# The Mamba branch's convolution projection: twelve column slabs regrouped into three groups of four slabs of two k tiles

## The chip, the cores and the metric

The kernel runs on one core of a Trainium2 chip. The metric is the device time of one execution in microseconds (us). A profiled execution has its own time; the profile's span is the stretch from its first to its last instruction.

## The reference

Four layers act on a sequence of 512 positions by 1024 features in fp32: two of a three-branch block (gated spatial mixing, Mamba2, differential attention, then a feed-forward network) and two of a second block. Only the first block's layers ("first layer" and "second layer" below) hold the code that is changed. What matters of them:

```python
h = rmsnorm(x, attn_norm_g[layer])
proj = h @ w_in[layer]                      # 1024 -> 8208 columns
gm_u, gm_v, ssm_z, ssm_xbc, ssm_dt, da_q, da_k, da_v, gates = split_cols(proj, IN_SIZES)
...
xbc = jax.nn.silu(causal_dwconv(xbc, conv_w, conv_b))    # 1536 columns, 4 taps along the sequence
dt = jax.nn.softplus(dt_raw.astype(jnp.float32) + dt_bias.astype(jnp.float32))
y = ssd_scan(xs..., dt, a_log, bm..., cm..., d_skip)
return rmsnorm(y * jax.nn.silu(z), norm_g)
```

## The kernel before, in words

**A weight slab's way.** All large products run through one pipeline of slabs of at most 128 partitions by 1024 words. SP loads slab s into one of four raw buffers (`load`, L550 to L553); it waits until slab s-4 is done on TensorE, because they share the buffer. ScalarE rounds it to a high part (`split_hi`, L565 to L569), VectorE subtracts to get the low part (`split_lo`, L571 to L575), and TensorE forms each product as three matmuls, high by high, high by low, low by high (`mm3`, L577 to L581). ScalarE and VectorE issue these two steps three slabs ahead (`hi_ahead` and `lo_ahead`, `LEAD = 3`) between their other work, each engine in one fixed order written out by hand. The slabs' order is a list (L320): gv 4, xbc 12, z 8, gu 4, gate_a 8, and so on. Slab names below count from 0: xbc 3 is the fourth slab of xbc.

**Two shapes of product.** `slab_t` (L588) takes a slab of all eight k tiles (of 128 input features) by 128 columns: 24 matmuls into one PSUM bank, which is complete when the slab is. `slab_n` (L609) takes a slab of two k tiles by 512 columns: each of four banks gets six matmuls from each of four slabs, and the four banks are complete one after the other while the fourth slab runs; `rows_done` (L637) counts the first three, `slab_done` the last, and `rows_filled` (L650) waits for them. With `features=True` its output tiles are 128 features by 512 positions, as those of `slab_t`. A slab is 24 matmuls in either shape. There are four banks in `pg`, used in turn (`take_bank`, L583), each free when its reader has counted up `bank_free`.

**The stretch that is changed.** In each of the first two layers TensorE runs gv (4 slabs, `slab_n`), the small dt projection (L2124 to L2144, one bank), xbc (12 slabs, `slab_t`, L2146 to L2151), z 0 to 3 (`slab_n` with features), and then waits for `dt_ready` (L2161) and transposes. The bank of dt is the one that the fourth output tile of xbc takes next. It is freed by VectorE's L1406. In the first layer VectorE waits before it for all fifteen parameter loads (L1400) and for the tables `c_pack` (L1401); SP issues those between the first xbc slabs, the tables last (L2615 to L2620). ScalarE waits for the parameters too (L915).

For each xbc tile ScalarE evicts the bank twice, as the first tap into `xb` (L849) and as a copy into `conv_in` (L850), and VectorE adds three more taps (L1417) from the copy, each after the one before. `conv_in` holds four tiles. In the kernel before, each engine does one tile and then the split of one slab, tile after tile, and the second and third group of four are a loop with a register. After the last tile and the low part of slab z 2, VectorE runs the chain of dt (L1430 to L1447: softplus by a series, with the low parts of z 3 and z 4 in between, and four scans), at whose end `dt_ready` is complete. ScalarE runs SiLU over `xb` (L937), and then evicts z's banks (L953).

The lines that the steps below touch:

```python
        def load(sp, s, m, it, dst, src):
            wait(sp, slab_done, count(s - RAW + 1, m, it))
            sp.dma_start(dst, src).then_inc(landed[s % RAW], 16)
...
                if l == 0:
                    dve.wait_ge(S("tables_landed"), 16)
                dve.wait_ge(S("dt_done"), past("dt_done") + 1)
```

Of the kernel before, what the change touches and what calls it, by code (L numbers as in the profile page):

```python
# [10 lines left out]
ACT = mybir.ActivationFunctionType  # L11
AX = mybir.AxisListType

P = 128
SEQ = 512
# [59 lines left out]
def count(c, m, it):  # L75

    if isinstance(it, int):
        return c + m * it
    return it * m + c

def wait(eng, sem, value):

    if isinstance(value, int) and value <= 0:
        return
    eng.wait_ge(sem, value)
# [27 lines left out]
def program(nc, t, out, depth=DEPTH, depth2=DEPTH):  # L114
    with ExitStack() as ctx:
# [13 lines left out]
        def S(name):  # L129

            if name not in sems:
                sems[name] = ctx.enter_context(nc.semaphore(name))
            return sems[name]
# [105 lines left out]
        def zf(i):  # L239
            return nb1[:, i // 2, GM_W + SEQ * (i % 2):GM_W + SEQ * (i % 2) + SEQ]  # L240
# [282 lines left out]
        def past(name):  # L523

            a, b = min(now[0], depth), max(now[0] - depth, 0)
            return a * PER1.get(name, 0) + b * PER2.get(name, 0)

        def groups_past():

            return 6 * min(now[0], depth) + 7 * max(now[0] - depth, 0)  # L530

# [286 lines left out]
        def unit_filled(eng, s, u, m=0, it=0):  # L818

            wait(eng, slab_done, count(s + 1, m, it))  # L820
            return pg[:, u % BANKS, :]
# [16 lines left out]
        def _(act):  # L838
            chain = Chain(act, "act_step")

            def hi_ahead(s, m=0, it=0):

                if s + LEAD < len(WORDS):
                    split_hi(act, s + LEAD, m, it, WORDS[s + LEAD + (m * it if isinstance(it, int) else 0)])

            def conv_first_tap(s, u, m, it, i, acc, w, b, j):

                bank = unit_filled(act, s, u, m, it)
                nc.scalar.activation(acc, bank, ACT.Identity, bias=b, scale=w)  # L849
                nc.scalar.activation(conv_in[:, j, 4:4 + SEQ], bank, ACT.Copy).then_inc(bank_free[u % BANKS], 1)  # L850
# [36 lines left out]
            for l in range(depth):  # L887
# [26 lines left out]
                nc.scalar.activation(gstat[:, 4:8], gstat[:, 0:4], ACT.Sqrt, bias=eps[:, :], scale=1.0 / GM_W).then_inc(S("gm_rms"), 1)  # L914
                act.wait_ge(S("par_landed"), past("par_landed") + 16 * 15)  # L915

                act.wait_ge(S("dt_x"), past("dt_x") + 1)
                act.wait_ge(S("dt_x"), past("dt_x") + 1)
# [4 lines left out]

                def xbc(it):
                    for j in range(4):
                        wait(act, S("conv_step"), past("conv_step") + count(3 * (j - 3), 12, it))
                        i = count(j, 4, it)
                        conv_first_tap(SL["xbc"] + j, UN["xbc"] + j, 4, it, j, xb[:, i, :] if isinstance(i, int) else xb[:, bass.ds(i, 1), :],
                                       conv_w[:, i, 3:4], conv_b[:, bass.ds(i, 1)], j)  # L930
                        hi_ahead(SL["xbc"] + j, 4, it)
                xbc(0)
                with act.Fori(1, 3) as it:
                    xbc(it)
                for j in range(3):
# [13 lines left out]
                def z_in(half):  # L949

                    s, u = SL["z"] + 4 * half, UN["z"] + 4 * half
                    for b in range(4):
                        nc.scalar.activation(zf(4 * half + b), rows_filled(act, s + 3, u, b, 1 + half), ACT.Silu).then_inc(bank_free[(u + b) % BANKS], 1)  # L953

# [61 lines left out]
                nc.scalar.activation(ystat[:, 0:TT], sums_of(pm_filled(act, u), TT), ACT.Sqrt, bias=eps[:, :], scale=1.0 / SSM_I).then_inc(pm_free[u % 4], 1)  # L1016
                rows_in(block(qkv, 0), SL["qkv"], UN["qkv"], 3)
                for c in range(3, 7):
                    hi_ahead(SL["qkv"] + c)
                rows_in(block(qkv, 1), SL["qkv"] + 4, UN["qkv"] + 4, 4)  # L1020
                for c in range(7, 10):
# [3 lines left out]
                hi_ahead(SL["qkv"] + 10)  # L1025
                rows_in(block(qkv, 2), SL["qkv"] + 8, UN["qkv"] + 8, 5)
                hi_ahead(SL["qkv"] + 11)
# [306 lines left out]
        def _(dve):  # L1334
# [44 lines left out]
            for l in range(depth):  # L1379
# [30 lines left out]

                def xbc(it):
                    for j in range(4):
                        unit_left(dve, UN["xbc"] + j, 4, it)
                        i = count(j, 4, it)
                        row = xb[:, i, :]
                        for b in range(1, SSM_K):
                            nc.vector.scalar_tensor_tensor(row, conv_in[:, j, 4 - b:4 - b + SEQ], conv_w[:, i, 3 - b:4 - b], row,  # L1417
                                                           ALU.mult, ALU.add).then_inc(S("conv_step"), 1)
                            if b < SSM_K - 1:
                                dve.wait_ge(S("conv_step"), past("conv_step") + count(3 * j + b, 12, it))  # L1420
                        lo_ahead(SL["xbc"] + j, 4, it)
                xbc(0)
                dve.wait_ge(S("gm_rms"), past("gm_rms") + 1)
                chain(nc.vector.reciprocal(gstat[:, 4:8], gstat[:, 4:8]))
                for tt in range(TT):
                    nc.vector.tensor_scalar(gv[:, tt, :], gv[:, tt, :], gstat[:, 4 + tt:5 + tt], None, ALU.mult).then_inc(S("gm_vn"), 1)
                with dve.Fori(1, 3) as it:
                    xbc(it)
# [647 lines left out]
        def _(pe):  # L2076
# [34 lines left out]
            for l in range(depth):  # L2111
# [33 lines left out]

                def xbc(it):  # L2146
                    for j in range(4):
                        slab_t(pe, SL["xbc"] + j, UN["xbc"] + j, 4, it, hh, hl, KD)
                xbc(0)
                with pe.Fori(1, 3) as it:  # L2150
                    xbc(it)  # L2151

# [398 lines left out]
        def _(sp):  # L2551
# [34 lines left out]
            def first_block(l):  # L2586
                def one(s, m, it, w, c):
                    load(sp, s, m, it, raw_view(s, KD, P), w_cols(w, l, c))

                def xbc(it):  # L2590
                    for j in range(4):
                        one(SL["xbc"] + j, 4, it, w_in, count(C_XBC + P * j, 4 * P, it))

                def rows512(s0, c0, n):
# [14 lines left out]
                if l == 0:  # L2609
                    for j in range(4):  # L2610
                        x_load(j)
                        gv_load(j)
                    dt_load(0)
                    sp.wait_ge(setup, 8)
                    params = params_of(0)  # L2615
                    load_params(params, 3)
                    for j in range(4):
                        one(SL["xbc"] + j, 0, 0, w_in, C_XBC + P * j)
                        load_params(params, 3)
                    sp.dma_start(c_pack[:, P:], t["c_pack"][:, P:]).then_inc(S("tables_landed"), 16)  # L2620
                    with sp.Fori(1, 3) as it:
                        xbc(it)
                    load_ffn_params(0)
                else:
                    for j in range(4):
                        gv_load(j)
                    with sp.Fori(0, 3) as it:
                        xbc(it)
                rows512(SL["z"], C_Z, 2)
# [112 lines left out]
```

## Time and profile before

| what | us |
|---|---|
| median of 3 runs | 2538.36 (2538.08 to 2539.93) |
| profiled execution, its own time | 2542.14 |
| its span | 2540.4 |
| TensorE busy | 2524.2 (99% of the span) |
| VectorE busy | 1588.0 (63%) |
| ScalarE busy | 1172.6 (46%) |
| GpSimd busy | 326.6 (13%) |

The profiled execution is 1.7 us longer than its span and 3.8 us longer than the median. In the rows PE is TensorE's matmul, PEld its weight load, DVE VectorE, ACT ScalarE, POOL GpSimd, SP SyncE, and SPq the queue of transfers that SP issues. L12 is line 12 of the kernel. A start is in us from the span's start. Of a transfer, "to landing" is the time from its issue on SP until all of it has arrived. Matmuls overlap: one that takes 0.39 us is followed by the next after some 0.23 us.

### The profile page before, as it was taken

Reading aid. Unit: us, or ns where it says so; the run is one execution under the profiler, and the core shown is the slowest. Engines: PE = TensorE matmul, PEld = TensorE weight load, DVE = VectorE, ACT = ScalarE, POOL = GpSimd, SP = SyncE. Lnnn points to the kernel's source line nnn. Section 1 sums busy time; section 2 is a strip of 40 time slices with the busy share of each in tenths; the row PEclk is TensorE's granted clock in tenths of the full one; section 3 lists DMA queues with packets and bytes.
Section 4 is the critical chain, followed back from the end, with each engine's and each line's share of the span. In section 5 each row is a group of like instructions: output and inputs, shape, how many; then the busy total and the mean of one; then the engine's idle time right before and its main releaser. Section 6 shows DMA issues by size and latency. Waiting matters only on the chain.

```text
span 2540.4 us, 34369 instructions
## 1 busy us (share of the span) xinstructions
PE 2524.2 (99%) x12345; PEld 2062.6 (81%) x12345; DVE 1588.0 (63%) x2458; ACT 1172.6 (46%) x2120; POOL 326.6 (13%) x256
## 2 busy tenths in 40 slices
PE   8999999999999999999999999999999999999999
PEld 7887887888888887887877888888888777887777
DVE  6745767567777336637666467775345677647765
ACT  6434545434433235336354444333246555575563
POOL 1024201010111001215020201110010001110010
PEclk9999999999999999999999999999999999999999
DMA  6443342333333455442343333333324322333322
GB/s 133 102 83 63 88 91 75 63 104 91 99 98 90 104 104 84 92 81 68 91 84 70 85 94 94 96 99 94 101 79 108 83 63 61 90 96 75 84 59 74
DMA packets 417918, 221.93 MB, mean 87 GB/s; under 512 B 52704, under 2 KB 400896, under 8 KB 417536
## 3 DMA queue, kind: packets, MB, share of 16 engines
q1 hardware_dynamic: 417792, 220.26, 35.8%
q8 instruction: 78, 1.28, 0.2%
q14 instruction: 48, 0.39, 0.1%
HBM read 218.12 MB, written 2.10 MB: 87 GB/s over the span
## 4 chain that ended last, share of the span: by engine, by line
PE 94%; SPq 2%; DVE 1%; DMA 1%; ACT 1%; issue 1%; DVEq 0%; ACTq 0%
PE pg L579 28%; PE pg L581 27%; PE pg L580 27%; PE pm L679 3%; PE pm L2444 1%; SPq L2579 1%; PE pm L2326 1%; DMA w_raw<-in_w_in_dram 1%; PE pm L2418 1%; PE pm L2276 1%; PE pm L2224 1%; DVE w_lo L574 1%; PE pm L2458 1%; PE pm L2485 1%; PE pm L2227 0%
## 5 line engine op out<-in xcount | busy, mean ns | idle before, releaser
L574 DVE TENSOR_TENSOR w_lo<-w_raw,w_hi 128x1024 fp32r<-128x1024 f32 (+3 forms) x440 | 540.6, 1229 | 508.2 <-ACT w_hi L569 506.1
L579 PE MATMUL pg<-h_hi,w_hi 128*128 128x512 f32 x1856 | 738.6, 398 | 5.1 <-DVE w_lo L574 4.8
L581 PE MATMUL pg<-h_hi,w_lo 128*128 128x512 f32 x1856 | 724.4, 390 | 0.0
L580 PE MATMUL pg<-h_lo,w_hi 128*128 128x512 f32 x1856 | 724.2, 390 | 0.0
L569 ACT ACTIVATE w_hi<-w_raw 128x1024 fp32r<-128x1024 f32 (+3 forms) x440 | 433.9, 988 | 555.5 <-DMA w_raw<-in_w_in_dram 215.5
L579 PEld LDWEIGHTS pg<-h_hi,w_hi 128*128 128x128 f32 x1856 | 349.4, 188 | 82.5 <-issue 11.0
L581 PEld LDWEIGHTS pg<-h_hi,w_lo 128*128 128x128 f32 x1856 | 349.2, 188 | 74.1
L580 PEld LDWEIGHTS pg<-h_lo,w_hi 128*128 128x128 f32 x1856 | 349.7, 188 | 69.2 <-issue 1.0
L579 PE MATMUL pg<-w_hi,h_hi 128*128 128x512 f32 (+2 forms) x440 | 164.0, 373 | 0.0
L580 PE MATMUL pg<-w_lo,h_hi 128*128 128x512 f32 (+2 forms) x440 | 162.0, 368 | 0.0
L581 PE MATMUL pg<-w_hi,h_lo 128*128 128x512 f32 (+2 forms) x440 | 161.9, 368 | 0.0
L1696 DVE SCALAR_TENSOR_TENSOR arena<-conv_in,par,arena 128x512 f32<-128x512 f32 x176 | 131.9, 749 | 15.2 <-DVE arena L1696 10.6
L579 PE MATMUL pg<-f_hi,w_hi 128*128 128x512 f32 x352 | 136.9, 389 | 0.0
L580 PE MATMUL pg<-f_lo,w_hi 128*128 128x512 f32 x352 | 136.9, 389 | 0.0
L581 PE MATMUL pg<-f_hi,w_lo 128*128 128x512 f32 x352 | 136.9, 389 | 0.0
L1120 ACT ACTIVATE arena<-conv_in,par 128x512 f32<-128x512 f32 x88 | 71.9, 817 | 125.9 <-DVE conv_in L1690 125.9
L563 POOL TENSOR_TENSOR f_lo<-arena,f_hi x44 | 56.9, 1293 | 518.1 <-DVE f_hi L1704 518.1
L1690 DVE TENSOR_TENSOR conv_in<-pg,rinv 128x512 f32<-128x512 f32 x88 | 60.8, 691 | 88.7 <-PE pg L581 79.5
L579 PE MATMUL pg<-nb_parts,w_hi 128*128 128x512 f32 x256 | 101.8, 398 | 0.0
L581 PE MATMUL pg<-nb_parts,w_lo 128*128 128x512 f32 x256 | 99.7, 390 | 0.0
L579 PEld LDWEIGHTS pg<-w_hi,h_hi 128*128 128x128 f32 x440 | 82.8, 188 | 12.7 <-issue 0.9
L581 PEld LDWEIGHTS pg<-w_hi,h_lo 128*128 128x128 f32 x440 | 82.9, 188 | 12.6
(410 smaller groups left out, 3753.4 us busy)
## 6 DMA issues: line engine op xcount, KB each, us to landing
w_raw<-in_w_in_dram SPq DMA_DIRECT2D x184, 512.0 KB, 5.0
w_raw<-in_ffn_w_up_dram SPq DMA_DIRECT2D x88, 512.0 KB, 3.6
w_raw<-in_w_out_dram SPq DMA_DIRECT2D x32, 512.0 KB, 3.8
w_raw<-in_ffn_w_down_dram SPq DMA_DIRECT2D x32, 512.0 KB, 3.8
w_raw<-in_w_branch_b_dram SPq DMA_DIRECT2D x16, 512.0 KB, 3.8
w_raw<-in_ffn_w_down_dram SPq DMA_DIRECT2D x16, 384.0 KB, 3.4
w_raw<-in_w_branch_a_dram SPq DMA_DIRECT2D x16, 256.0 KB, 2.8
w_raw<-in_w_branch_c_dram SPq DMA_DIRECT2D x16, 256.0 KB, 2.8
```

The source lines that it names most:

```text
L563: return nc.gpsimd.tensor_tensor(lo, value, hi.bitcast(F32), ALU.subtract)
L569: nc.scalar.activation(w_hi[:, s % HI, 0:n], w_raw[:, s % RAW, 0:n], ACT.Copy).then_inc(hi_done, 1)
L574: nc.vector.tensor_tensor(w_lo[:, s % RAW, 0:n], w_raw[:, s % RAW, 0:n], w_hi[:, s % HI, 0:n].bitcast(F32), ALU.subtract)\
L579: nc.tensor.matmul(dst, l_hi, r_hi, start=start, stop=False)
L580: nc.tensor.matmul(dst, l_hi, r_lo, start=False, stop=False)
L581: return nc.tensor.matmul(dst, l_lo, r_hi, start=False, stop=stop)
L679: done = nc.tensor.transpose(dst, src, ident[0:src.shape[0], 0:src.shape[0]])
L1120: nc.scalar.activation(facc[:, j, :], conv_in[:, j, 4:4 + SEQ], ACT.Identity, bias=fconv_b[:, bass.ds(i, 1)], scale=fconv_w[:, i, 2:3]).th ...
L1690: nc.vector.tensor_tensor(conv_in[:, j, 4:4 + SEQ], unit_filled(dve, SL["up"] + j, UN["up"] + j, 4, it), inv[:, :], ALU.mult)\
L1696: nc.vector.scalar_tensor_tensor(facc[:, j, :], conv_in[:, j, 4 - a:4 - a + SEQ], fconv_w[:, i, 2 - a:3 - a], facc[:, j, :], ALU.mult, ALU ...
L2224: done = nc.tensor.matmul(bank[rows, c * P:(c + 1) * P], xdt[:, c, h * 64:h * 64 + 64], seg[:, h % 4, c, :], start=True, stop=c == 0)
L2276: done = nc.tensor.matmul(bank[:, kt * P:SEQ], qkv[:, kt, 1024 + h * P:1024 + (h + 1) * P], wt(h, kt), start=kt == 0, stop=kt == TT - 1)
```

## The change

The twelve xbc slabs of each layer become three groups of four slabs of two k tiles by 512 columns. TensorE runs `slab_n(..., features=True)` for them, four output tiles at once. SP loads 2 x 128 rows by 512 columns for each (pieces of 2 KB) in place of 8 x 128 rows by 128 columns (pieces of 512 B). ScalarE evicts four tiles in a row at each group's end (with the high parts of up to three slabs ahead of them), VectorE does the low parts of three slabs, the taps of two tiles, one low part, and the taps of two tiles. The loops with a register are written out. The counts of `rows_done` of the later groups move up by three in each layer. In both layers the high part of xbc 3 is made ahead of ScalarE's wait for `dt_x`. The data, the number of matmuls and of other instructions stay the same.

```diff
-            return 6 * min(now[0], depth) + 7 * max(now[0] - depth, 0)
+            return 9 * min(now[0], depth) + 7 * max(now[0] - depth, 0)
...
-            def conv_first_tap(s, u, m, it, i, acc, w, b, j):
-
-                bank = unit_filled(act, s, u, m, it)
+            def conv_first_tap(bank, u, acc, w, b, j):
+
                 nc.scalar.activation(acc, bank, ACT.Identity, bias=b, scale=w)
                 nc.scalar.activation(conv_in[:, j, 4:4 + SEQ], bank, ACT.Copy).then_inc(bank_free[u % BANKS], 1)
...
                 act.wait_ge(S("par_landed"), past("par_landed") + 16 * 15)
-
-
-                act.wait_ge(S("dt_x"), past("dt_x") + 1)
+                hi_ahead(SL["xbc"])
+
                 act.wait_ge(S("dt_x"), past("dt_x") + 1)
...
-                def xbc(it):
+                for it in range(3):
+                    s, u = SL["xbc"] + 4 * it, UN["xbc"] + 4 * it
+                    for j in range(1 if it == 0 else 0, 3):
+                        hi_ahead(s + j)
                     for j in range(4):
-                        wait(act, S("conv_step"), past("conv_step") + count(3 * (j - 3), 12, it))
-                        i = count(j, 4, it)
-                        conv_first_tap(SL["xbc"] + j, UN["xbc"] + j, 4, it, j, xb[:, i, :] if isinstance(i, int) else xb[:, bass.ds(i, 1), :],
-                                       conv_w[:, i, 3:4], conv_b[:, bass.ds(i, 1)], j)
-                        hi_ahead(SL["xbc"] + j, 4, it)
-                xbc(0)
-                with act.Fori(1, 3) as it:
-                    xbc(it)
+                        i = 4 * it + j
+                        wait(act, S("conv_step"), past("conv_step") + 12 * it + 3 * (j - 3) if i >= 4 else 0)
+                        conv_first_tap(rows_filled(act, s + 3, u, j, 1 + it), u + j, xb[:, i, :], conv_w[:, i, 3:4], conv_b[:, i:i + 1], j)
+                    hi_ahead(s + 3)
...
                 def xbc(it):
+
+                    s, u = SL["xbc"] + 4 * it, UN["xbc"] + 4 * it
+                    for j in range(3):
+                        lo_ahead(s + j)
                     for j in range(4):
-                        unit_left(dve, UN["xbc"] + j, 4, it)
-                        i = count(j, 4, it)
-                        row = xb[:, i, :]
+                        i = 4 * it + j
+                        unit_left(dve, u + j)
                         for b in range(1, SSM_K):
...
-                        lo_ahead(SL["xbc"] + j, 4, it)
+                        if j == 1:
+                            lo_ahead(s + 3)
                 xbc(0)
...
-                def xbc(it):
+                for it in range(3):
                     for j in range(4):
-                        slab_t(pe, SL["xbc"] + j, UN["xbc"] + j, 4, it, hh, hl, KD)
-                xbc(0)
-                with pe.Fori(1, 3) as it:
-                    xbc(it)
+                        slab_n(pe, SL["xbc"] + 4 * it, UN["xbc"] + 4 * it, hh, hl, 512, 4, 2, j, features=True)
...
                     for j in range(4):
-                        one(SL["xbc"] + j, 0, 0, w_in, C_XBC + P * j)
+                        load(sp, SL["xbc"] + j, 0, 0, raw_view(SL["xbc"] + j, 2, 512), w_block(w_in, l, 2 * P * j, 2 * P, C_XBC, 512))
                         load_params(params, 3)
                     sp.dma_start(c_pack[:, P:], t["c_pack"][:, P:]).then_inc(S("tables_landed"), 16)
-                    with sp.Fori(1, 3) as it:
-                        xbc(it)
+                    rows512(SL["xbc"] + 4, C_XBC + 512, 2)
                     load_ffn_params(0)
```

## Rows read from the trace of the kernel before

**Rows 1.** the page, part 1 (busy us, share of the span, instructions)

```profile
...
PE 2524.2 (99%) x12345; PEld 2062.6 (81%) x12345; DVE 1588.0 (63%) x2458; ACT 1172.6 (46%) x2120; POOL 326.6 (13%) x256
...
```

**Rows 2.** waits of PE alone, 30 to 1100 us: total us, times, longest us

```profile
...
PE pg L579 <- DVE w_lo L574: 4.8, 2, 2.7
...
```

**Rows 3.** timeline of PE, first layer (start us, us)

```profile
...
41.49 0.39 PE L579 MATMUL pg<-h_hi,w_hi 128*128 128x512 f32 x1
...
45.57 0.39 PE L579 MATMUL pg<-h_hi,w_hi 128*128 128x512 f32 x1
...
60.66 0.80 PE L579 MATMUL pg<-h_hi,w_hi 128*128 128x512 f32 x1 [2.68 <-DVE w_lo L574]
...
```

**Rows 4.** timeline of PE, second layer

```profile
...
1001.31 0.49 PE L579 MATMUL pg<-h_hi,w_hi 128*128 128x512 f32 x1 [2.16 <-DVE w_lo L574]
...
```

**Rows 5.** windows: busy by engine, granted clock, DMA share, GB/s

```profile
...
60.60:67.70 7.10, 7.04 (x25) 5.74 (x26) 6.60 (x9) 1.74 (x3) 0.00 (x0) 0.79 0.38 99
...
1001.30:1008.80 7.50, 7.49 (x26) 6.05 (x27) 6.89 (x11) 2.82 (x4) 0.00 (x0) 0.77 0.50 62
38.00:44.00 6.00, 5.22 (x23) 3.09 (x22) 5.22 (x6) 5.90 (x8) 2.70 (x3) 1.00 0.06 3
...
```

**Rows 6.** DMA issues, 971.5 to 1014.5 us (count, KB, median us to landing)

```profile
...
w_raw<-in_w_in_dram SPq DMA_DIRECT2D x8, 512.0 KB, 8.4
```

**Rows 7.** DMA issues, 1019.5 to 1057 us

```profile
...
w_raw<-in_w_in_dram SPq DMA_DIRECT2D x7, 512.0 KB, 4.2
```

**Rows 8.** the page, part 6: issues, KB each, median us to landing

```profile
...
w_raw<-in_w_out_dram SPq DMA_DIRECT2D x32, 512.0 KB, 3.8
...
```

**Rows 9.** timeline of DVE, first layer

```profile
...
51.28 0.74 DVE L1405 TENSOR_SCALAR arena<-pg,par 16x512 f32<-16x512 f32 x1 [7.65 <-DMA c_pack<-in_c_pack_dram]
52.06 0.68 DVE L1406 TENSOR_TENSOR arena<-arena,pg 16x512 f32<-16x512 f32 x1
...
57.14 2.33 DVE L1417 SCALAR_TENSOR_TENSOR arena<-conv_in,par,arena 128x512 f32<-128x512 f32 x3 [3.96 <-ACT conv_in L850]
59.38 1.22 DVE L574 TENSOR_TENSOR w_lo<-w_raw,w_hi 128x1024 fp32r<-128x1024 f32 x1
...
```

**Rows 10.** timeline of SP's issues, first layer

```profile
...
32.29 4.50 SPq L2579 DMA_DIRECT2D par<-in_ssm_d_dram  x2
...
38.03 3.99 SPq L2579 DMA_DIRECT2D par<-in_ssm_a_log_dram  x1
...
44.53 1.24 SPq L2620 DMA_DIRECT2D c_pack<-in_c_pack_dram  x1
```

**Rows 11.** timeline of SP's issues, end of the first layer

```profile
...
884.57 0.65 SPq L2579 DMA_DIRECT2D par<-in_ssm_d_dram  x1
...
```

**Rows 12.** DMA issues, 31.5 to 32.2 us

```profile
...
w_raw<-in_w_in_dram SPq DMA_DIRECT2D x1, 512.0 KB, 7.2
...
```

**Rows 13.** timeline of ACT, second layer

```profile
...
1036.11 0.78 ACT L849 ACTIVATE arena<-pg,par 128x512 f32 x1 [3.22 <-PE pg L581]
1036.79 0.59 ACT L850 ACTIVATE conv_in<-pg 128x512 f32<-128x512 f32 x1
1037.27 1.06 ACT L569 ACTIVATE w_hi<-w_raw 128x1024 fp32r<-128x1024 f32 x1
...
1057.63 0.60 ACT L953 ACTIVATE arena<-pg 128x512 f32<-128x512 f32 x1 [0.76 <-PE pg L581]
...
```

**Rows 14.** timeline of DVE, second layer

```profile
...
1041.24 0.41 DVE L1431 TENSOR_SCALAR arena<-arena 16x512 f32<-16x512 f32 x1
...
1055.43 1.36 DVE L1447 TENSOR_TENSOR_SCAN rms<-consts,arena 16x128 f32<-16x128 f32 x4
...
```

**Rows 15.** timeline of PE, end of the first z group

```profile
...
1057.52 0.41 PE L679 MATMUL pm<-c_pack,arena 16*128 16x16 f32 x4
...
```

**Rows 16.** timeline of ACT, first layer

```profile
...
106.72 1.06 ACT L569 ACTIVATE w_hi<-w_raw 128x1024 fp32r<-128x1024 f32 x1 [4.81 <-DMA w_raw<-in_w_in_dram]
...
111.53 0.78 ACT L849 ACTIVATE arena<-pg,par 128x512 f32 x1 [1.64 <-PE pg L581]
...
```

More of the change, by code:

```diff
@@ L952, in z_in @@
                     for b in range(4):
-                        nc.scalar.activation(zf(4 * half + b), rows_filled(act, s + 3, u, b, 1 + half), ACT.Silu).then_inc(bank_free[(u + b) % BANKS], 1)
+                        nc.scalar.activation(zf(4 * half + b), rows_filled(act, s + 3, u, b, 4 + half), ACT.Silu).then_inc(bank_free[(u + b) % BANKS], 1)
                 hi_ahead(SL["z"] + 2)
@@ L1016, in _ @@
                 nc.scalar.activation(ystat[:, 0:TT], sums_of(pm_filled(act, u), TT), ACT.Sqrt, bias=eps[:, :], scale=1.0 / SSM_I).then_inc(pm_free[u % 4], 1)
-                rows_in(block(qkv, 0), SL["qkv"], UN["qkv"], 3)
+                rows_in(block(qkv, 0), SL["qkv"], UN["qkv"], 6)
                 for c in range(3, 7):
                     hi_ahead(SL["qkv"] + c)
-                rows_in(block(qkv, 1), SL["qkv"] + 4, UN["qkv"] + 4, 4)
+                rows_in(block(qkv, 1), SL["qkv"] + 4, UN["qkv"] + 4, 7)
                 for c in range(7, 10):
@@ L1025, in _ @@
                 hi_ahead(SL["qkv"] + 10)
-                rows_in(block(qkv, 2), SL["qkv"] + 8, UN["qkv"] + 8, 5)
+                rows_in(block(qkv, 2), SL["qkv"] + 8, UN["qkv"] + 8, 8)
                 hi_ahead(SL["qkv"] + 11)
@@ L1411, in xbc @@
                 def xbc(it):
+                    s, u = SL["xbc"] + 4 * it, UN["xbc"] + 4 * it
+                    for j in range(3):
+                        lo_ahead(s + j)
                     for j in range(4):
-                        unit_left(dve, UN["xbc"] + j, 4, it)
-                        i = count(j, 4, it)
-                        row = xb[:, i, :]
+                        i = 4 * it + j
+                        unit_left(dve, u + j)
                         for b in range(1, SSM_K):
-                            nc.vector.scalar_tensor_tensor(row, conv_in[:, j, 4 - b:4 - b + SEQ], conv_w[:, i, 3 - b:4 - b], row,
+                            nc.vector.scalar_tensor_tensor(xb[:, i, :], conv_in[:, j, 4 - b:4 - b + SEQ], conv_w[:, i, 3 - b:4 - b], xb[:, i, :],
                                                            ALU.mult, ALU.add).then_inc(S("conv_step"), 1)
                             if b < SSM_K - 1:
-                                dve.wait_ge(S("conv_step"), past("conv_step") + count(3 * j + b, 12, it))
-                        lo_ahead(SL["xbc"] + j, 4, it)
+                                dve.wait_ge(S("conv_step"), past("conv_step") + 3 * i + b)
+                        if j == 1:
+                            lo_ahead(s + 3)
                 xbc(0)
@@ L1426, in _ @@
                     nc.vector.tensor_scalar(gv[:, tt, :], gv[:, tt, :], gstat[:, 4 + tt:5 + tt], None, ALU.mult).then_inc(S("gm_vn"), 1)
-                with dve.Fori(1, 3) as it:
+                for it in (1, 2):
                     xbc(it)
@@ L2588, in one @@
                     load(sp, s, m, it, raw_view(s, KD, P), w_cols(w, l, c))
-                def xbc(it):
-                    for j in range(4):
-                        one(SL["xbc"] + j, 4, it, w_in, count(C_XBC + P * j, 4 * P, it))
                 def rows512(s0, c0, n):
@@ L2626, in first_block @@
                         gv_load(j)
-                    with sp.Fori(0, 3) as it:
-                        xbc(it)
+                    rows512(SL["xbc"], C_XBC, 3)
                 rows512(SL["z"], C_Z, 2)
```

## The prediction

> **What bounds the kernel now.** I read the page first: TensorE is busy for 2524.2 of the span's 2540.4 us [rows 1], so a change that removes no matmul can win only where TensorE waits, and must lose wherever it makes TensorE wait. Next come the waits of TensorE in the stretch that holds both layers' xbc groups: two for a slab's low part, 4.8 us together [rows 2], and otherwise 1 us. They are the upside. TensorE's timeline places them: the first layer's at xbc 3, until 60.66 us [rows 3], the second's at xbc 6, until 1001.31 us [rows 4]. So the first wait costs 2.7 + 1.5 = 4.2 us and the second 2.2 + 1.7 = 3.9 us. Of three tiles in 45.57 - 41.49 = 4.08 us [rows 3] each takes 1.36 us and a slab 5.44 us; that pace stays, since the matmuls are the same ones.
>
> **Step 1, second layer, transfers: -3.9 us.** Around the second layer's wait eight xbc slabs land 8.4 us (median) after their issue [rows 6]. The seven transfers behind them, nearly all z slabs, read the same matrix with the same row distance, but in pieces of 2 KB, and land after 4.2 us [rows 7]. With raw buffers handed back four slabs behind, a slab has three slabs, 16.3 us, for landing and both splits, and xbc 6 missed that. The change gives xbc the shape of z. I take 4.2 us and let the whole wait go with its clock: -3.9 us. The bounds are nothing and -3.9 us, as no other wait stands here.
> The Trainium skill (DMA: Bandwidth & Descriptors, Specifications) gives 512 B as the smallest transfer for line rate, so the old pieces should already be good enough and this step would bring nothing. The row of w_out, cut into 512 B as well, agrees with it at 3.8 us [rows 8]; the row of xbc does not. The matrix is the difference between them, and for this matrix I go by z's row.
>
> **Step 2, first layer, the bank of dt: +1.9 us.** Now TensorE needs xbc 3 only in the fourth slab, but all four banks in the first. The fourth bank is that of dt. TensorE asks for it after three tiles, at 45.57 us [rows 3], where it used to ask some 16 us after the start. VectorE frees it with L1406, and stands before that until the tables have landed: it starts at 51.28 us, and the second addition ends at 52.06 + 0.68 = 52.74 us [rows 9], 1.46 us after the start. What is queued behind this wait on VectorE are the low parts and all taps; on TensorE everything. With the tables landing as before, TensorE would wait 7.1 us, plus 1.6 us of clock, against the 4.2 us that go (the old wait was for the low part of xbc 3, which stood behind ScalarE's first eviction and three taps, 57.14 to 59.38 us [rows 9], and now comes ahead of them): +4.5 us, the upper bound.
> Do the tables land sooner? SP issues them at 44.53 us, behind 4.50 us for two ssm_d transfers and 3.99 us for a_log [rows 10], where an unhindered one takes 0.65 us [rows 11]; meanwhile, from 38 to 44 us, the engines of DMA are busy for 0.06, one in sixteen, at 3 GB/s [rows 5]. So a small, serial transfer (ssm_d by its place) holds up all that is behind it, and it waits itself for xbc 2 ahead of it, which takes 7.2 us to land [rows 12]. At 4.2 us [rows 7] it lands 3.0 us sooner. I take 2.7 us of that for the tables: start 48.6, bank free 50.0, a wait of 4.5 us, and 4.5 + 1.6 - 4.2 = +1.9 us. Were all of SP's hold-ups gone (3.3 us on a_log, some 1.2 us more behind it), the start would be near 46.7 us, the wait 2.6 us, the step 0: the lower bound.
> In the second layer the parameters came in during the first, and VectorE frees this bank just before it is asked for; I cost that at nothing.
>
> **Step 3, the end of xbc: +3.7 us in the second layer, +4.1 us in the first.** Call T the end of the last xbc slab. In the second layer ScalarE starts its last eviction at T = 1036.11, has the copy 1.27 us later, and goes on 1.16 us after the start [rows 13]; VectorE begins the chain of dt at 1041.24, T + 5.1, and ends its scans at 1055.43 + 1.36 = 1056.79 [rows 14], 15.55 us on. TensorE starts its transposes at 1057.52 [rows 15], 0.1 us before ScalarE has z's last tile (1057.63 [rows 13]): the cover is 0.7 us thin.
> After the change the four tiles of the last group end at T - 4.08, T - 2.72, T - 1.36 and T. The first copy is there at T - 2.8. Taps of one tile take 59.38 - 57.14 = 2.24 us where nothing is a register [rows 9], so two tiles end at T + 1.7. The low part of z 2 waits for ScalarE's four evictions and one high part, T + 1.16 + 1.06 = T + 2.2 [rows 13], and ends at T + 3.4; two tiles more, T + 7.9. The chain is the same, so dt is ready at T + 7.9 + 15.55 = T + 23.45, where TensorE wants it at T + 21.4: 2.1 us of waiting. What is late is the taps, not the matmuls: four tiles' taps used to be spread over four slabs, and now pile up behind the group. TensorE's idle of 2.16 us cost 1.7 us of clock [rows 4, 5], and this is its nearest row: 2.1 + 1.6 = 3.7 us. Without the fall it would be 2.1 us.
> In the first layer ScalarE must also make z 1's high part before it evicts, and z 0's alone, late because of the feed-forward parameters on the same queue, started at 106.72, T - 4.8 with T = 111.53 [rows 16]. Two high parts of 1.06 us end at T - 2.7, 1.4 us after the first tile. Some of that goes with the shorter queue; I add 0.4 us, bounds 0 and 1.4.
> Groups one and two have the same pile, but no chain behind it: the next low part is due 16 us later. SiLU (L937) ends near T + 10 and is covered by z's 21.8 us. The written-out loops save registers' work on VectorE and ScalarE, which TensorE does not wait for. Moving xbc 3's high part ahead costs nothing, since ScalarE was waiting there. The transfers in number and bytes are the same, SP's queue is passed by nothing new.
>
> **The sum.** -3.9 + 1.9 + 4.1 + 3.7 = +5.8 us: 2542.1 becomes 2547.9 in a profiled execution like this one. The shown median lies 3.8 us below the profiled time; the difference carried over to it gives 2538.4 + 5.8 = 2544.2 us. All steps at their low ends (0, 2.1 and 2.1 us, no fall of clock) give +0.3 us, at their high ends (4.5, 5.1, 3.7) +9.4 us, and the transfers' gain absent +9.7 us.
>
> **The rivals.** (a) The waits come as said, but both are too short for the clock to fall: 5.8 - 3.2 = +2.6 us, 2541.0. For it: the idle is a shade under 2.16 us, and what follows is small transposes. Against it: both idles of over 2 us in these stretches brought a fall. It cannot be told from no change.
> (b) The second layer's wait stays, because the slow landings come from the matrix and not from the pieces: +9.7 us, 2548.1. The skill's 512 B rule from step 1 would have it so. Against it stands z with half the time in the same stretch.
> (c) The tables land near 46.7 us, and the bank of dt costs nothing on balance: +3.9 us, 2542.3.
> (d) The other side: VectorE's pile at the end of xbc stays hidden. That needs dt ready by T + 21.4, 2.1 us sooner than my sum, as it would be if the scans' end and not the taps set it, or the low part of z 2 found its high part ready. Then -3.9 + 1.9 = -2.0 us, 2536.4; it decides from the point at which the chain starts before T + 5.8. Against it: four tiles are 9 us of taps on one engine in order, and they cannot start before T - 2.8.
> That the change doesn't do what it says is hardly possible: the counts of rows_done fit the three new groups.
>
> **How the numbers follow.** About 0.2%, 5 us, is what a measurement of this kernel can tell from no change. The forecast has 0.45, and its own range is +3 to +9.4 us; (a) 0.27, (b) 0.08, (c) 0.10, (d) 0.10. Slower by over 5 us holds three quarters of the forecast, all of (b) and a little of (a) and (c): 0.47. Faster by as much needs (d) and (c) together and more: 0.05. The rest, 0.48, is within. The range of 8 in 10 leaves out the lower part of (d) and the upper part of (b): 2537.4 to 2548.4 us.
>
> **What would show it.** In the profile after: a wait of TensorE of 3 to 7 us near 46 us, ended by VectorE's L1406 (step 2); none near 999 us, and xbc slabs landing in 4 to 5 us (step 1); a wait of 2 to 3 us before L679 at the end of each first z group, with VectorE starting L1431 near T + 8 (step 3), and a lower granted clock behind each of the three. I am wrong if the tables land before 46 us, if L1431 starts before T + 6, or if the second layer still waits for xbc's low part.

## The result, and the profile after

The changed kernel takes 2546.09 us (median of 7 runs, 2544.11 to 2548.13), the kernel before 2538.36 us (7 runs, 2535.62 to 2539.93): a ratio of 1.0031, 95% interval 1.0019 to 1.0043. That is 7.7 us slower, where 5.8 us were forecast; 2546.1 lies inside the range of 2537.4 to 2548.4. The profiled executions differ by less: their spans are 2544.4 and 2540.4 us. Why that is so is half of what follows.

The page of the changed kernel, parts 1 and 6 [rows 1, 8]:

```profile
PE 2524.6 (99%) x12345; PEld 2062.7 (81%) x12345; DVE 1587.9 (62%) x2458; ACT 1174.7 (46%) x2120; POOL 325.4 (13%) x256
...
w_raw<-in_w_out_dram SPq DMA_DIRECT2D x32, 512.0 KB, 3.9
```

TensorE has the same work, 2524.6 against 2524.2 us, so the difference must lie in where it stands still or runs at its lower clock. Its waits from 30 to 1100 us [rows 2]:

```profile
PE pg L579 <- DVE arena L1403: 4.9, 1, 4.9
PE pm L679 <- DVE rms L1448: 3.6, 2, 1.8
PE pg L2135 <- POOL h_lo L563: 0.6, 1, 0.6
```

Both waits for `w_lo` are gone; the bank of dt (freed by L1403, which was L1406) and dt's scans (L1448, was L1447) have taken their place. TensorE's timeline at the three places, the first three lines from the first layer [rows 3, 4]:

```profile
50.95 0.79 PE L579 MATMUL pg<-h_hi,w_hi 128*128 128x512 f32 x1 [4.89 <-DVE arena L1403]
...
137.38 0.42 PE L679 MATMUL pm<-c_pack,arena 16*128 16x16 f32 x4 [1.80 <-DVE rms L1448]
...
139.47 0.63 PE L580 MATMUL pg<-h_lo,w_hi 128*128 128x512 f32 x1
...
1061.05 0.42 PE L679 MATMUL pm<-c_pack,arena 16*128 16x16 f32 x4 [1.81 <-DVE rms L1448]
...
1063.05 0.39 PE L580 MATMUL pg<-h_lo,w_hi 128*128 128x512 f32 x1
```

The two waits for the scans are alike to 0.01 us, but what follows is not: the same 128x512 matmul takes 0.63 us behind the first and 0.39 us behind the second. The windows say the same (TensorE's busy time, granted clock, DMA share, GB/s) [rows 5]:

```profile
48.00:58.00 10.00, 7.05 (x25) 0.83 0.28 58
...
130.00:140.00 10.00, 8.20 (x46) 0.96 0.50 106
140.00:150.00 10.00, 10.00 (x44) 0.87 0.14 30
1000.00:1010.00 10.00, 10.00 (x46) 1.00 0.37 107
1055.00:1065.00 10.00, 8.19 (x47) 1.00 0.53 106
```

A fall to 1.2 GHz costs 10 x 0.17 = 1.7 us after the bank's wait and 10 x (0.04 + 0.13) = 1.7 us after the first layer's scans; in the second layer there is none.

**Why the bank is late**, in VectorE's timeline and SP's [rows 9, 10], with the issue of xbc 3 in the second fence:

```profile
49.44 0.74 DVE L1402 TENSOR_SCALAR arena<-pg,par 16x512 f32<-16x512 f32 x1 [5.47 <-DMA c_pack<-in_c_pack_dram]
50.22 0.68 DVE L1403 TENSOR_TENSOR arena<-arena,pg 16x512 f32<-16x512 f32 x1
```

```profile
32.15 1.41 SPq L2577 DMA_DIRECT2D par<-in_ssm_d_dram  x2
33.59 0.63 SPq L2577 DMA_DIRECT2D par<-in_ssm_dt_bias_dram  x1
37.17 0.38 SPq L553 DMA_DIRECT2D w_raw<-in_w_in_dram  x1
37.59 0.47 SPq L2577 DMA_DIRECT2D par<-in_ssm_a_log_dram  x1
38.10 4.17 SPq L2577 DMA_DIRECT2D arena<-in_gm_w_s_dram  x1
...
42.86 0.43 SPq L2614 DMA_DIRECT2D c_pack<-in_c_pack_dram  x1
```

The tables are issued at 42.86 us in place of 44.53, and VectorE gets on at 49.44 in place of 51.28. Little of this comes from ssm_d. Its two issues take 3.1 us less, but SP then stands from 34.22 to 37.17 us until TensorE is done with the buffer that xbc 3 needs. In the kernel before it issued xbc 3 at 37.56 us, without such a wait, so only 0.4 us of the 3.1 get past this point. The rest of the tables' gain is made behind it: a_log takes 0.47 us for 3.99, gm_w_s 4.17 us for 1.81, and the sum is 0.4 + 3.5 - 2.4 = 1.5 of the 1.7 us.

**Why dt is late**, first layer, ScalarE's evictions and VectorE's work behind them [rows 13, 14, 16]:

```profile
109.83 0.78 ACT L848 ACTIVATE arena<-pg,par 128x512 f32<-128x512 f32 x1 [1.21 <-PE pg L581]
...
113.92 0.78 ACT L848 ACTIVATE arena<-pg,par 128x512 f32<-128x512 f32 x1
```

```profile
111.14 4.57 DVE L1417 SCALAR_TENSOR_TENSOR arena<-conv_in,par,arena 128x512 f32<-128x512 f32 x6 [1.25 <-ACT conv_in L849]
116.16 1.23 DVE L574 TENSOR_TENSOR w_lo<-w_raw,w_hi 128x1024 fp32r<-128x1024 f32 x1 [0.46 <-ACT w_hi L569]
117.31 4.56 DVE L1417 SCALAR_TENSOR_TENSOR arena<-conv_in,par,arena 128x512 f32<-128x512 f32 x6
121.78 0.41 DVE L1432 TENSOR_SCALAR arena<-arena 16x512 f32<-16x512 f32 x1
...
135.97 1.36 DVE L1448 TENSOR_TENSOR_SCAN rms<-consts,arena 16x128 f32<-16x128 f32 x4
```

This is the forecast pile: two tiles' taps, a low part, two tiles' taps, and only then the chain. With T = 113.92, the start of the last eviction, the chain starts at T + 7.86 (forecast T + 7.9) and dt is ready at 137.33 = T + 23.41 (forecast T + 23.45). TensorE wants it at 137.38 - 1.80 = T + 21.66 (forecast T + 21.4), so the wait is 1.8 us and not 2.1.

**The transfers.** From 971.5 to 1014.5 us xbc now lands in 4.7 us, against 8.4 [rows 6]:

```profile
w_raw<-in_w_in_dram SPq DMA_DIRECT2D x7, 512.0 KB, 4.7
```

The median of before hides the slab that matters. Its xbc 6 alone, issued at 982.8 us:

```profile
w_raw<-in_w_in_dram SPq DMA_DIRECT2D x1, 512.0 KB, 16.0
```

With a high part of 1.06 and a low part of 1.23 us behind the landing that makes 18.3 us, against the 16.3 us that three slabs give: 2.0 us too late, for a wait of 2.16 us. By the same sum a landing of 8.4 us would have been in time.

### The profile page after: what moved, and what is told of

It reads as the page before. It is cut to its first block, busy times and chain, and to the rows that moved or that the text cites. A ratio compares the mean times of both kernels' runs of the same rounds, so it can differ in the third digit from the quotient of the medians.

```text
span 2544.4 us, 34125 instructions
## 1 busy us (share of the span) xinstructions
PE 2524.6 (99%) x12345; PEld 2062.7 (81%) x12345; DVE 1587.9 (62%) x2458; ACT 1174.7 (46%) x2120; POOL 325.4 (13%) x256
## 4 chain that ended last, share of the span: by engine, by line
PE 95%; DVE 3%; issue 1%; DMA 1%; ACT 0%; SPq 0%; DVEq 0%; ACTq 0%
PE pg L579 28%; PE pg L581 28%; PE pg L580 28%; PE pm L679 3%; PE pm L2442 1%; DVE w_lo L574 1%; PE pm L2324 1%; PE pm L2416 1%; PE pm L2274 1%; PE pm L2222 1%; PE pm L2456 1%; PE pm L2483 1%; PE pm L2225 0%; PE pm L2205 0%; PE pm L2197 0%
```

## The experiments

My theory after the result: the new grouping costs what the two new waits and the clock behind them take, less the old waits. The rivals: the new pieces or order cost something by themselves; or what the trace of before showed is not what the kernel before usually does.

### The change in one layer only

```diff
-                for it in range(3):
+                for it in range(3) if grouped() else ():
```

The same switch stands in the program of each engine that the change touches, the old loops in its other arm; `grouped()` is true for the first layer in one kernel, for the second in the other.

> Only the first layer has the new grouping; the second is as before. My account (bank of dt, then taps piled up ahead of the chain of dt): the first layer alone costs 6.2 us, as the two traces have it (2.7 at the bank, 3.4 at the end of the first z group with its fall of the clock); the second layer's wait for xbc 6 is there as before. So 2538.4 + 6.2 = 2544.6 us. Rival: the loss lies in the second layer or is spread over the kernel by the written-out loops; then this is half of it at most, under 2542 us.

Measured: 2544.57 us (7 runs, 2543.78 to 2547.26), ratio 1.0027 (1.0016 to 1.0039).

> Only the second layer has the new grouping. By the two traces it brings 4.2 us of transfers back and loses 1.9 us ahead of L679: 2538.4 - 2.3 = 2536.1 us. Rival: the second layer's wait for xbc 6 is not in every execution of the kernel before (its profiled execution is 3.8 us over the median); then nothing is won and this is 2538.4 + 1.9 = 2540.3 us, and first and second together add up to the measured 7.7 us.

Measured: 2539.48 us (11 runs, 2537.3 to 2541.49), ratio 1.0007 (0.9998 to 1.0016). Waits from 30 to 1100 us, the first-layer kernel, then the second-layer one:

```profile
PE pg L583 <- DVE arena L1419: 4.7, 1, 4.7
PE pg L583 <- DVE w_lo L578: 2.2, 1, 2.2
PE pm L683 <- DVE rms L1482: 1.8, 1, 1.8
```

```profile
PE pg L583 <- DVE w_lo L578: 3.0, 1, 3.0
PE pm L683 <- DVE rms L1482: 1.8, 1, 1.8
```

The first layer is as I said. The second came out 3.4 us above my account and 0.8 us below its rival: in the median, the second layer's change brings no gain that covers its new wait. Step 1 is in doubt. The first layer's old wait, left in this kernel, is 3.0 us here and no lower clock follows it.

### The chain of dt cut in three

The chain of dt, L1432 to L1448, is cut in three and run behind the first low part of groups 0, 1 and 2 of xbc, so that it no longer stands behind the last taps.

```diff
+                def dt_part(it):
+                    if it == 0:
+                        dve.wait_ge(S("dt_exp"), past("dt_exp") + 1)
...
                     for j in range(3):
                         lo_ahead(s + j)
+                        if j == 0:
+                            dt_part(it)
```

> The changed kernel with VectorE's chain of dt cut in three and run in the gaps of groups one, two and three, right behind the first low part of each, in place of behind the last taps. If the pile of taps ahead of the chain is what delays the transposes, both waits for L1448 (1.8 us each) and the fall of the clock behind the first go: 2546.1 - 5.3 = 2540.8 us, with L679 directly behind the matmuls. Rival: SiLU on ScalarE or the low parts of z take their place as the last to come; then a wait of over 1 us stays ahead of L679 and the gain is under 2 us.

Measured: 2541.33 us (11 runs, 2539.74 to 2542.06), ratio 1.0014 (1.0005 to 1.0023). The only wait left:

```profile
PE pg L579 <- DVE arena L1403: 4.9, 1, 4.9
```

4.8 us under the changed kernel's 2546.09, where 5.3 were expected, and 3.9 us under its median in a later series (2545.18, below). Both waits and the lower clock behind them are gone: the cause that step 3 names is shown, its size for the two layers together to about 1 us.

### The bank of dt freed before the wait for the tables

```diff
+                dve.wait_ge(S("dt_done"), past("dt_done") + 1)
+                chain(nc.vector.tensor_copy(dt_t, pg[0:SSM_H, UN["dt"] % BANKS, :]))
+                nc.vector.tensor_tensor(dt_t, dt_t, pg[2 * SSM_H:3 * SSM_H, UN["dt"] % BANKS, :], ALU.add).then_inc(bank_free[UN["dt"] % BANKS], 1)
...
-                chain(nc.vector.tensor_scalar(dt_t, pg[0:SSM_H, UN["dt"] % BANKS, :], dt_b[0:SSM_H, :], None, ALU.add))
-                nc.vector.tensor_tensor(dt_t, dt_t, pg[2 * SSM_H:3 * SSM_H, UN["dt"] % BANKS, :], ALU.add).then_inc(bank_free[UN["dt"] % BANKS], 1)
+                chain(nc.vector.tensor_scalar(dt_t, dt_t, dt_b[0:SSM_H, :], None, ALU.add))
```

> The changed kernel with the bank of dt freed ahead of VectorE's waits for parameters and tables (a copy and an addition out of PSUM, then the waits, then the bias; one small instruction more). If the bank is what TensorE waits for at 46 us, its 4.9 us and the fall of the clock behind it (1.5 us) go: 2546.1 - 6.4 = 2539.7 us. Rival: the tables' lateness still counts by another way (low part of xbc 3, the taps), and a wait of 3 us or more comes up within the first group; then the gain is under 3 us.

Measured: 2539.04 us (11 runs, 2537.02 to 2540.73), ratio 1.0008 (0.9999 to 1.0017). That is 7.0 us under the changed kernel's first median and 6.1 under the later one, where 6.4 were expected. The bank's wait is gone and nothing took its place; the scans' two waits remain:

```profile
PE pm L679 <- DVE rms L1449: 3.6, 2, 1.8
```

### Both together

> The new grouping with both pile-ups taken away: the bank of dt freed before the wait for the tables, and the chain of dt cut in three, run behind the first low part of groups 0, 1 and 2. My account (the waits for the bank and for dt's scans are all that the new grouping costs, and they are independent): the two single changes came out 4.8 and 7.0 us under the changed kernel, so 2546.1 - 11.8 = 2534.3 us, some 4 us under the kernel before, no wait of TensorE over 1 us between 30 and 1100 us and no stretch of lower clock there. Rival (one of the two only moves its time to a wait behind it, such as the low part of xbc 3 or the tables' later users): 2538 to 2540 us, with a new wait near 50 or 135 us.

Measured: 2534.07 us (11 runs, 2533.17 to 2534.38), ratio 0.9984 (0.9975 to 0.9993). It beats both kernels, the one before by 4.1 us. All that stands in TensorE's list of waits from 30 to 1100 us:

```profile
PE pg L2144 <- POOL h_lo L563: 0.6, 1, 0.6
PE pg L606 <- DVE m_lo L1674: 0.4, 1, 0.4
```

VectorE frees the bank at 45.09 us, before it stands for the tables, which come no sooner than in the changed kernel but no longer hold up TensorE:

```profile
44.41 0.68 DVE L1399 TENSOR_TENSOR arena<-arena,pg 16x512 f32<-16x512 f32 x1
49.38 0.47 DVE L1405 TENSOR_SCALAR arena<-arena,par 16x512 f32<-16x512 f32 x1 [4.30 <-DMA c_pack<-in_c_pack_dram]
```

The runs also spread over 1.2 us only, against 4.3 us of the kernel before in its first 7. That suggests that most of what made single executions differ was the stalls.

### Is it the size of the pieces?

The changed kernel, each xbc slab fetched by four transfers:

```diff
+                    for a in range(4):
+                        sem = landed[sl % RAW] if a == 3 else pieces_in[sl % RAW]
+                        sp.dma_start(raw_view(sl, 2, 512)[:, :, P * a:P * a + P], w_block(w_in, l, 2 * P * j, 2 * P, C_XBC + 512 * it + P * a, P)).then_inc(sem, 16)
```

> The changed kernel, but each xbc slab fetched as four transfers of 128 columns, so in pieces of 512 B again, the order of the work unchanged. If the size of the pieces made the old landings of 8.4 us, xbc slabs of the second layer take about 8 us again from first issue to landing (12 in a row, against 4 us in the changed kernel), the second layer's wait for a low part can come back, and the time is 2546 to 2550 us. Rival (b) of the prediction (the matrix or its neighbours in the queue, not the pieces): 4 to 5.5 us, of which up to 1.5 us is that four issues follow one another, and 2546 us.

And the kernel before, cut in four as well, but with the slab's shape kept:

```diff
+                    for a in range(4):
+                        sem = landed[sl % RAW] if a == 3 else pieces_in[sl % RAW]
+                        sp.dma_start(raw_view(sl, KD, P)[:, 2 * a:2 * a + 2, :], w_block(w_in, l, 2 * P * a, 2 * P, count(C_XBC + P * j, P * m, it), P)).then_inc(sem, 16)
```

> The kernel before, but each xbc slab (eight k tiles by 128 columns) fetched as four transfers of two k tiles; pieces, bytes and number of transfers as in the run on pieces, only that the 512 B pieces of a slab lie in 1024 rows of the matrix and not side by side in 256. If it is the place of the pieces (narrow columns over many rows) that makes the old landings of 8.4 us, the slabs of the second layer still take about 8 us from first issue to landing and the last of the four transfers clearly more than 4 us. If it was that one transfer held all 1024 pieces, they land in 5 to 6 us as in the run on pieces. Time 2538 us in either case, as the second layer's wait is not in every execution.

Transfers issued from 971.5 to 1014.5 us, the changed kernel in 512 B pieces, then the kernel before in four:

```profile
w_raw<-in_w_in_dram SPq DMA_DIRECT2D x28, 128.0 KB, 3.5
```

```profile
w_raw<-in_w_in_dram SPq DMA_DIRECT2D x30, 128.0 KB, 5.4
```

Each transfer has the same 256 pieces of 512 B, and takes 3.5 against 5.4 us. Over the twelve slabs of the second layer, from a slab's first issue to its last landing, the medians are 5.3 and 7.5 us (mostly 1.4 to 1.7 us of it is issuing four). So pieces of 512 B are good enough where a slab's four transfers lie side by side in the same 256 rows, and slow where they go down 1024 rows. (The two kernels also lay the pieces out differently in the raw buffer; that was not varied by itself.) The prediction's reason, "in pieces of 2 KB", was wrong, its number nearly right. The Trainium skill's 512 B rule (DMA: Bandwidth & Descriptors, Specifications), which I had set aside, agrees with 3.5 us and cannot explain 5.4.

The changed kernel's own trace has more on this, since it still reads several matrices as 1024 rows of 512 B. First the twelve slabs of w_in issued from 1067 to 1140 us, then ffn_w_up in the whole span, then 23 slabs of the second block's own input matrix, issued from 1932 to 2085 us, which the profile also calls in_w_in:

```profile
w_raw<-in_w_in_dram SPq DMA_DIRECT2D x12, 512.0 KB, 8.0
...
w_raw<-in_ffn_w_up_dram SPq DMA_DIRECT2D x88, 512.0 KB, 3.7
...
w_raw<-in_w_in_dram SPq DMA_DIRECT2D x23, 512.0 KB, 3.7
```

The slabs have one shape, and the rows of the matrices lie 32,832, 22,528 and 17,024 B apart; those of w_out lie 4096 B apart and its slabs take 3.8 us [rows 8]. Of four row distances only the largest is slow. The same page of the Trainium skill (Latency and other measured facts) reports row distances of large powers of two as slow; this one is 64 B over 32 KiB, smaller than those it measured. No run changed the distance for one matrix, so what makes w_in slow stays open.

The times: 2548.47 us (5 runs; ratio 1.0042, 1.0028 to 1.0056) and 2536.03 us (10 runs; 0.9994, 0.9984 to 1.0004). The second is 2 us under what was expected, within what can be told from no change. The first is 2.4 us over the changed kernel. In its trace the four issues of xbc 3 hold SP for 5.98 us, which pushes the tables from 42.86 back to 45.34 us, and the bank's wait grows from 4.9 to 6.1 us; the lower clock behind it costs 3.4 us in place of 1.7, in this one execution.

```profile
PE pg L585 <- DVE arena L1409: 6.1, 1, 6.1
```

### Does standing still make the clock fall?

The changed kernel, with TensorE busy where it waits for dt's scans:

```diff
+                bank = take_pm(pe, PM["dt_n"])
+                for _ in range(14):
+                    nc.tensor.transpose(bank[:, 0:P], ident, ident)
```

> The changed kernel with 14 transposes of the identity on TensorE in the place where it waits 1.8 us for dt's scans, their result overwritten. If the idle itself makes the clock fall behind it, no stretch of lower clock follows near 139 us and the time is 2546.1 - 1.7 = 2544.4 us, at most 2543 us if executions mostly show the fall in both layers. If the fall has nothing to do with TensorE standing idle there (it was absent in the second layer after the same wait), the clock is lower near 139 us again and the time is 2546.1 us.

Measured: 2545.31 us (8 runs, 2543.87 to 2545.73), ratio 1.0029 (1.0018 to 1.004). The wait is 0.27 us in the first layer, and the clock stays up behind it, as the second window shows:

```profile
138.72 0.42 PE L679 MATMUL pm<-c_pack,arena 16*128 16x16 f32 x4 [0.27 <-DVE rms L1448]
...
140.95 0.39 PE L581 MATMUL pg<-h_hi,w_lo 128*128 128x512 f32 x1
```

```profile
48.00:58.00 10.00, 7.22 (x19) 0.66 0.28 60
...
140.00:150.00 10.00, 10.00 (x52) 1.00 0.25 59
```

That is what would come if the idle itself made the clock fall, but it shows little. The kernel with the change in the first layer only had the full wait at the same place, and its clock stayed up as well (the window's 1.00, behind the busy times of all five engines):

```profile
138.31 0.41 PE L683 MATMUL pm<-c_pack,arena 16*128 16x16 f32 x4 [1.79 <-DVE rms L1482]
...
140.00:150.00 10.00, 10.00 (x50) 8.39 (x50) 6.41 (x11) 1.06 (x1) 9.09 (x6) 1.00 0.23 56
```

The median moved by only 0.8 us, and not at all against the later series of the changed kernel (2545.18). The clock behind the bank's wait fell for twice as long in this execution (10 x 0.34 = 3.4 us). So the run decides neither the time nor the mechanism.

### The kernels themselves, run again

> The kernel before itself, for a second profiled execution. Its first one lay 3.8 us over the median of its runs. If the second layer's wait of 2.2 us for the low part of xbc 6 with its 1.7 us of clock belongs to some executions only, this profile comes without it at 2538 us; if it belongs to all, it is there again and the time is 2538 to 2542 us.

> The kernel before, for a third profiled execution: whether the second layer's wait for the low part of xbc 6 is there in one execution of three or in two. With it 2540 to 2542 us, without it 2536 to 2538 us; in both the xbc slabs of the second layer land after 8 us.

> The changed kernel itself, for a second profiled execution. The waits come from order and durations and should be there again: 4.9 us for the bank of dt, 1.8 us for dt's scans in either layer. The lower clock behind them changed from place to place in the runs so far (3.4 or 6.8 us behind the bank's wait, behind the scans' in one layer, both or none); if it is a matter of the execution and not of the kernel, it falls otherwise here, and the span goes with it by 1.7 us for each 3.4 us at the lower level: 2542.7 to 2547.8 us.

Measured: the kernel before 2537.67 us (8 runs, ratio to itself 0.9998, 0.9988 to 1.0008) and, in a single run, 2536.52 us; the changed one 2545.18 us (5 runs, ratio 1.0032, 1.0019 to 1.0045). Waits from 30 to 1100 us in the second and in the third profiled execution of the kernel before [rows 2]:

```profile
PE pg L579 <- DVE w_lo L574: 3.3, 1, 3.3
```

```profile
PE pg L579 <- DVE w_lo L574: 2.1, 2, 1.5
```

The second has no such wait in the second layer at all, the third one of 0.5 us (2.1 less 1.5) and no lower clock. The slow landings are there every time (8.3 and 8.1 us in the stretch of [rows 6]). What differs is xbc 6 itself: it landed after 16.0 us in the first profile, 12.2 in the second and 14.4 in the third. With 2.3 us for its two parts against a slack of 16.3 us that is 2.0 us too late, in time, and 0.4 us too late. The changed kernel's waits come back:

```profile
PE pg L579 <- DVE arena L1403: 4.3, 1, 4.3
PE pm L679 <- DVE rms L1448: 3.6, 2, 1.8
```

### One account for all thirteen traces

From each profiled span I take TensorE's waits at these places (for the bank of dt, for dt's scans, for xbc's low parts), and 1.7 us for about each 0.17 that a 10 us window is short of a clock of 1.00, from 30 to 1100 us. In the filled kernel the transposes stand in for 3.1 us of waiting:

| profiled execution | span | waits | clock | rest |
|---|---|---|---|---|
| before, first | 2540.4 | 4.8 | 3.4 | 2532.2 |
| before, second | 2536.6 | 3.3 | 1.7 | 2531.6 |
| before, third | 2534.8 | 2.1 | 0 | 2532.7 |
| changed, first | 2544.4 | 8.5 | 3.4 | 2532.5 |
| changed, second | 2543.3 | 7.9 | 3.4 | 2532.0 |
| first layer only | 2545.5 | 8.7 | 5.1 | 2531.7 |
| second layer only | 2538.6 | 4.8 | 1.7 | 2532.1 |
| chain in three | 2539.8 | 4.9 | 3.4 | 2531.5 |
| bank early | 2538.7 | 3.6 | 3.4 | 2531.7 |
| both early | 2532.4 | 0 | 0 | 2532.4 |
| 512 B pieces | 2546.8 | 9.7 | 5.1 | 2532.0 |
| wait filled | 2543.8 | 5.4 + 3.1 filled | 3.4 | 2531.9 |
| before, in four | 2534.6 | 2.4 | 0 | 2532.2 |

The rest is 2531.5 to 2532.7 us whatever the grouping, the pieces or the number of transfers. So a cost or a gain of grouping or pieces by themselves, apart from the stalls, is at most about 1 us, which is what the rest varies by.

## Why the prediction was right, and where its steps were off

The sign is right and the time is 1.9 us off, but the closeness is partly luck: step 1 took off 3.9 us that are not in the median, and step 3 put on 2.5 us too many.

**Step 1, -3.9 us: the term of the sum that failed.** It set the median landing of eight slabs, 8.4 us, beside the slack of 16.3 us and concluded that xbc 6 "missed that". The numbers do not give it: what missed was one landing of 16.0 us. The wait was "at xbc 6, until 1001.31 us", with "the whole wait ... with its clock" taken as the kernel's. In the first profile it does go, for 2.2 + 1.7 us. But three profiled executions of before show 2.2, 0 and 0.5 us there, so by these three there is mostly little to win. The kernel with the new second layer alone says so too: 1.6 us over the kernel before as it was timed beside it (2539.48 against 2537.9), with an interval that shuts out the 2536.1 of my account. I had the warning in hand: the profiled execution lay 3.8 us over the shown median, and I carried that difference over whole, as if it belonged to both kernels. The traces suggest that it was mostly this stall, which the change removes; the changed kernel's profile lies on its median (2546.09 both). The landings themselves were forecast at 4.2 us and took 4.7 in that stretch.

**Step 2, +1.9 us: right in kind and nearly in size, by a path that was wrong.** The bank was to come free at 50.0 us and came at 50.22 + 0.68 = 50.90; the wait is 4.9 us for a forecast 4.5. "2.7 us of that for the tables" was 1.8 us (51.28 to 49.44), and it did not come from ssm_d. SP's wait for xbc 3's buffer let only 0.4 us of ssm_d's 3.1 through; the shorter a_log, less the longer gm_w_s, brought the rest. The prediction passed over that wait in its own estimate, though its lower bound (3.3 + 1.2 us) fits it. Against the first trace the step is 4.9 + 1.7 - (2.7 + 1.7) = +2.2 us. Freeing the bank early took 7.0 or 6.1 us off, by which median of the changed kernel one takes; the wait and its clock are 6.6 us. The old wait that is set against it is also a sample: 2.7, 3.3 and 1.5 us in the three profiles of before, the last without a fall of the clock.

**Step 3, +4.1 and +3.7 us: right in mechanism, over-sized in clock.** "2.1 us of waiting" is 1.80 and 1.81 us, because TensorE arrived at T + 21.66 and not T + 21.4. The 0.4 us added for ScalarE in the first layer did not come: both high parts were done 1.2 us before the first eviction, as its idle before it shows. The clock, 1.6 us each, fell in the first layer and not in the second. Measured 3.5 + 1.8 = 5.3 us where 7.8 were summed; with the chain cut in three, 4.8 us went.

Against the first profile the steps make -3.9 + 2.2 + 3.5 + 1.8 = +3.6 us, measured +4.0. To the medians some 3.8 us come on top, by which that one execution of before lay over its median: 4.0 + 3.8 = 7.8, measured 7.7.

**The rivals.** (a), no fall of clock, held at one of the three places in the first profile. (b), slow landings because of the matrix and not the pieces: the landings went down to 4.7 us and the wait is gone, so it did not happen; the time alone could not exclude it, as +9.7 us lies inside the interval of the ratio (up to +10.9). Its premise is half right: the size of the pieces was not the cause. (c), tables at 46.7 us: they came at 49.44. (d), the pile stays hidden: excluded by the chain's start at T + 7.86, and reached on purpose by cutting the chain.

## What to carry to other kernels

A stall seen in one profiled execution is an estimate with one sample: where the profiled time stands off the median of the runs by as much as the stall is worth, the stall may not be in the median, and a gain from removing it must not be counted in full. When outputs of a projection are computed four at a time, everything that hangs on an output arrives in a burst at the group's end: look at what stands behind it in order on the evicting and the post-processing engine, and at how early the group needs its fourth bank. Both costs went by moving work that needed nothing new (an addition ahead of a wait, a chain between low parts), and only then was the change worth having. Whether these two moves alone, without the new grouping, would have brought as much was not run.

## What the runs showed of the hardware that was not expected

- **Between 1.8 and 3.0 us the length of an idle did not decide whether the clock fell.** Of the fifteen waits of TensorE of 1.8 to 3.0 us that the thirteen traces hold between 30 and 1100 us eight were followed by 1.2 GHz and seven were not: 1.8 us did it in the first layer and not in the second of the same execution, and 3.0 us once did not. All seven of 3.3 us and over, still between 30 and 1100 us, were followed by it, some at a cost of 1.7 us, some of 3.4. The Trainium skill (TensorE: Matmul & The Clock Gate, Part 1) says that the gate's window is free-running, so that the moment of a change depends on where in it the work falls; the traces are in keeping with that, and no run here varied it on purpose. The prediction took two idles, of 2.7 and 2.2 us, for a rule.
- **Where 512 B pieces lie matters more than that they are 512 B**: 3.5 against 5.4 us for 128 KB of w_in, and for a slab of one shape 8.0 us out of w_in against 3.7 us out of ffn_w_up, above.
- **A hold-up on SP's queue moves on.** Ssm_d's two issues fell from 4.50 to 1.41 us and a_log's from 3.99 to 0.47, but gm_w_s behind them rose from 1.81 to 4.17; with xbc 3 in four transfers it was their issues that took 5.98 us, and gm_w_s 0.55. What holds SP up in these places was not found: xbc 3 itself lands after 10.4 us in both kernels, in pieces of 512 B and of 2 KB.
